# Three chained blocks: the first product of a stage runs on the unnormed input and the norm's factor is put on its results

## What is computed

```python
def rmsnorm(x, g):
    y = xf * lax.rsqrt(jnp.mean(xf * xf, axis=-1, keepdims=True) + EPS)
    return y * g

# block 1
h = rmsnorm(x, ln_in_g); proj = h @ w_in        # its first 2048 columns: conv_a
...
x = x + y @ w_out
x = rmsnorm(x, final_g)
# block 2
h = rms_norm(x, norm1_g); proj = h @ w_in_2     # its first 2048 columns: q (sa_q)
...
x = x + merged @ w_out_2
h2 = rms_norm(x, norm2_g)
ff = square(relu(h2 @ w_ff1))
x = x + ff @ w_ff2
x = rms_norm(x, final_g_2)
# block 3
h = rms_norm_3(x, g_pre); proj = h @ w_in_3     # r and k of the scan: rwkv_rk
...
```

## Time and profile before

| what | value |
|---|---|
| median of 3 runs | 4041.4 us (4035.34 to 4043.63) |
| profiled execution | 4041.27 us, its span 4039.3 us |
| TensorE / its weight loads busy | 96% / 94% of the span |
| VectorE / ScalarE busy | 61% / 44% |
| DMA | 636.69 MB, mean 158 GB/s |
| instructions | 86905 |

### The profile page before, as it was taken

One profiled execution on the slowest core, in us unless ns is written; L12 is line 12 of the kernel. 1 busy time (PEld: TensorE's weight loads), 2 busy tenths in 40 slices (PEclk: granted clock), 3 DMA queues, 4 the chain that ended last, 5 costly groups with the idle time before them and its releaser, 6 DMA issues. The chain is left out here.

```text
span 4039.3 us, 86905 instructions
## 1 busy us (share of the span) xinstructions
PE 3889.9 (96%) x36410; PEld 3805.7 (94%) x36410; DVE 2484.2 (61%) x3560; ACT 1787.6 (44%) x2267; POOL 0.2 (0%) x4
## 2 busy tenths in 40 slices
PE   7999999999999899999999999999899999999998
PEld 7999999999998899999998999999899888899897
DVE  4699966876646653667645545455647665666465
ACT  3444444444444443466344434343345433345643
POOL 0000000000000000000000000000000000000000
PEclk9999999999999998999999999999999999999999
DMA  5555545435555464544554555555554311134454
GB/s 175 175 182 185 180 137 178 139 123 190 183 170 167 160 202 169 167 155 158 167 188 156 184 181 184 180 185 180 174 195 154 113 44 45 44 116 142 154 188 135
DMA packets 99405, 636.69 MB, mean 158 GB/s; under 512 B 11152, under 2 KB 14608, under 8 KB 28752
## 3 DMA queue, kind: packets, MB, share of 16 engines
q1 hardware_dynamic: 99120, 632.57, 47.5%
HBM read 624.10 MB, written 8.42 MB: 157 GB/s over the span
## 5 line engine op out<-in xcount | busy, mean ns | idle before, releaser
L310 PE MATMUL ps_gemm<-arena_r,w_hi 128*128 128x256 f32 x16576 | 2198.5, 285 | 41.5 <-DVE arena_r L649 17.2
L310 PEld LDWEIGHTS ps_gemm<-arena_r,w_hi 128*128 128x128 f32 x16576 | 2080.5, 192 | 58.7 <-issue 40.8
L256 DVE TENSOR_TENSOR ring_r<-ring,w_hi 128x1024 fp32r<-128x1024 f32 (+3 forms) x1264 | 1415.9, 1125 | 1055.1 <-ACT w_hi L250 1047.1
L250 ACT ACTIVATE w_hi<-ring 128x1024 fp32r<-128x1024 f32 (+3 forms) x1264 | 1229.7, 978 | 1208.0 <-PE ps_gemm L310 966.1
L310 PE MATMUL ps_gemm<-arena_r,ring_r 128*128 128x256 f32 x8288 | 1188.2, 284 | 22.9 <-DVE ring_r L256 22.0
L310 PEld LDWEIGHTS ps_gemm<-arena_r,ring_r 128*128 128x128 f32 x8288 | 1077.3, 192 | 33.4 <-DVE ring_r L256 31.2
L307 PE MATMUL ps_gemm<-w_hi,arena_r 128*128 128x256 f32 (+1 forms) x1408 | 192.2, 287 | 1.0 <-ACT w_hi L250 0.9
L1224 DVE SCALAR_TENSOR_TENSOR arena<-arena,vecs (+15 forms) x480 | 192.5, 466 | 0.0
L307 PEld LDWEIGHTS ps_gemm<-w_hi,arena_r 128*128 128x128 f32 x1408 | 181.1, 197 | 2.4 <-ACT w_hi L250 1.8
L467 ACT ACTIVATE arena<-ps_gemm 128x512 f32 (+2 forms) x99 | 59.1, 597 | 235.8 <-PE ps_gemm L310 188.2
L488 ACT ACTIVATE act_tmp<-ps_gemm 128x512 f32<-128x512 f32 x78 | 46.5, 596 | 167.9 <-PE ps_gemm L310 167.8
(11 more groups left out here) (335 smaller groups left out, 2296.8 us busy)
## 6 DMA issues: line engine op xcount, KB each, us to landing
ring<-in_ff SPq DMA_DIRECT2D x128, 1024.0 KB, 5.0
ring<-in_w_out SPq DMA_DIRECT2D x48, 1024.0 KB, 5.1
ring<-in_gate SPq DMA_DIRECT2D x32, 1024.0 KB, 5.1
ring<-in_conv_a SPq DMA_DIRECT2D x16, 1024.0 KB, 5.1
ring<-in_conv_b SPq DMA_DIRECT2D x16, 1024.0 KB, 5.1
ring<-in_gla_v SPq DMA_DIRECT2D x16, 1024.0 KB, 5.1
ring<-in_conv_z SPq DMA_DIRECT2D x16, 1024.0 KB, 5.0
ring<-in_conv_out SPq DMA_DIRECT2D x16, 1024.0 KB, 5.1
```

The source lines that it names most:

```text
L250: nc.scalar.activation(w_hi[q % 2][:, 0:size], ring[slot][:, part], ACT.Copy).then_inc(hi_ready, 1)
L256: nc.vector.tensor_tensor(ring_lo[slot][:, part], ring[slot][:, part], w_hi[q % 2][:, 0:size].bitcast(F32), ALU.subtract).then_inc(lo_read ...
L310: mm = nc.tensor.matmul(bank[0:cw, 0:T], w[:, k * cols + c * cw:k * cols + (c + 1) * cw], r[:, kk, :], start=start, stop=stop)
```

## The change

It does the same at four places: the opening (conv_a), sa_q of block 2, ff1_0, and rwkv_rk of block 3.

- The first product there (the lead) runs on gain x input, without the factor per token. Its input is split beside the units of the product before (`feeds` in `Prod`: per unit two ScalarE copies with the gain as scale, two VectorE remainders), at the opening as x arrives.
- The factor is put on the results: kind "scaled" (VectorE, PSUM times the factor, 8 units each of conv_a, sa_q, rwkv_rk, in place of a ScalarE copy), or, in all 32 ff1 units, a second multiplication in "relu2" by 1 / (mean + eps).
- The sum matmuls (`add_up`) stand behind quarter 1 of the lead's unit 0, at the opening behind quarter 3.
- The normed and split input for the later products is made beside units 1 to 5 of the lead (`first_product`); the once-normed residual beside units 4 to 7. The feed-forward needs no normed input (`feed_forward`).
- Table loads of blocks 2 and 3 are issued behind the lead's weights. All stages are one program Block; tables are placed at fixed addresses.
- Each epilogue also waits for the epilogue before it (`bank_free`).

```diff
+                if s.feeds:
+                    act.wait_ge(bank_free, i2 + (s.g0 + j + 3))
+                    for c in range(2):
+                        x, hi = (b[:, bass.ds(2 * i2 + (2 * j + c), 1), :].rearrange("p a t -> p (a t)") for b in (s.dst, s.feeds[0]))
+                        a = nc.scalar.activation(hi, x, ACT.Identity, scale=s.feed_gain(2 * i2 + (2 * j + c)))
+                    a.then_inc(split_hi, 1)
                 if s.sums is not None:
...
+                if s.feeds:
+                    dve.wait_ge(split_hi, i2 + (s.split0 + j + 1))
+                    for c in range(2):
+                        x, hi, lo = (b[:, bass.ds(2 * i2 + (2 * j + c), 1), :].rearrange("p a t -> p (a t)") for b in (s.dst, *s.feeds[0:2]))
+                        a = nc.vector.scalar_tensor_tensor(out=lo, in0=x, scalar=s.feed_gain(2 * i2 + (2 * j + c)), in1=hi.bitcast(F32), op0=ALU.mult, op1=ALU.subtract)
+                    a.then_inc(split_done, 1)
...
+                if s.kind == "scaled":
+                    dve.wait_ge(quarters_done, 4 * i2 + (4 * (s.g0 + j) + 4))
+                    nc.vector.scalar_tensor_tensor(out=d, in0=ps, scalar=s.scale, in1=by_token(2), op0=ALU.mult, op1=ALU.mult).then_inc(bank_free, 1)
+                    return
...
                 elif s.kind == "relu2":
-                    last = nc.vector.tensor_tensor(d, t, t, ALU.mult)
+                    nc.vector.tensor_tensor(tmp2[slot][:, :, :], t, t, ALU.mult).then_inc(dve_mid, 1)
+                    dve.wait_ge(dve_mid, i2 + (s.mid0 + j + 1))
+                    last = nc.vector.tensor_tensor(d, tmp2[slot][:, :, :], by_token(2), ALU.mult)
...
+        def first_product(lead, then, gain, src, split, sums, factors, opening=None, mid=None, loads=(), dve_body=None):
...
                 @block.scalar
                 def _(act):
+                    if opening:
+                        opening.act(act)
+                    lead.act_part(act, 0, 0)
+                    lead.act_part(act, 0, 1)
+                    lead.act_part(act, 0, 2)
+                    lead.act_part(act, 0, 3)
                     root(act, b_in + 1, outer)
-                    parts.act(act)
-                    root(act, b_in + 2, inner)
-                    run.act(act)
+                    if mid:
+                        root(act, b_in + 2, inner)
+                    for u in range(1, lead.n):
+                        lead.act_part(act, u, 0)
+                        lead.act_part(act, u, 1)
+                        if 1 < u < 6:
+                            act.wait_ge(split_in, parts.made0 + u - 1)
+                            nc.scalar.activation(parts.hi(u - 2), parts.raw(u - 2), ACT.Copy).then_inc(split_hi, 1)
+                        lead.act_part(act, u, 2)
+                        lead.act_part(act, u, 3)
...
+                    for q in range(4):
+                        lead.pe_quarter(pe, 0, q)
+                        if q == 1 and not opening:
+                            sums.add_up(pe)
+                    if opening:
+                        opening.add_up(pe)
...
+                    lead.dve_part(dve, 0, 0)
+                    lead.dve_part(dve, 0, 1)
+                    lead.dve_part(dve, 0, 2)
+                    rest_of_weights(dve, 0, lead.g0 + 1, 1)
+                    dve.wait_ge(sums_done, b_sums + (1 if opening else 0))
...
+            def act(s, act):
+                act.sem_inc(bank_free, 2)
+                act.wait_ge(s.vecs_in, 16)
+                for q in range(4):
+                    act.wait_ge(s.x_in[q], 16)
+                    for c in range(4 * q, 4 * q + 4):
+                        x = nc.scalar.activation(s.split[0][:, c, :], s.x[:, c, :], ACT.Identity, scale=vcol(s.gain, c))
+                    x.then_inc(split_hi, 1)
+                    if q < 2:
+                        round_weights(act, 0, 0, q)
+                for q in range(4):
+                    nc.scalar.activation(s.squares[:, 4 * q:4 * q + 4, :], s.x[:, 4 * q:4 * q + 4, :], ACT.Square).then_inc(sq_ready, 1)
```

382 lines of the change are left out of this document (209 added, 173 removed).

## The result

The changed kernel takes 3986.42 us (median of 4 runs, 3984.14 to 3989.21), the kernel before 4041.33 us (4 runs, 4035.34 to 4043.63). The ratio is 0.9867 with a 95% interval of 0.985 to 0.9884. The forecast was 3990.6 us, 4.2 us too high. The profiled execution of the changed kernel took 3989.21 us, its span 3987.4 us, 51.9 us under the span before.

The account below looks back on a forecast made before the run. TensorE was taken to bound the kernel, its pauses at four places being what could go. Gains of 7.8 + 14.8 + 13.2 + 14.9 = 50.7 us off 4041.3 gave 3990.6 us, eight in ten within 3982 to 4001.

Parts of the forecast that it names:

- The reading of the profile: Whole kernel: TensorE busy 3889.9 of 4039.3 us, so only fewer matmuls or less of its 149 us standing still pay.
- Block 1 to 2 and 2 to 3: At sa_q and rwkv_rk: 17.6 and 17.7 us lost before, gains of 14.8 and 14.9 us after sums and one wait.
- The wait for the rest of unit 1's quarter 3: Unit 1 of sa_q: VectorE has this rest at +11.5, TensorE wants it at 10.56, so it waits 1.0 us.
- (a): Lead units too full: units 1 to 5 each make TensorE wait 1 us at three places; 4004 us, chance 0.11.
- (d): Sum matmuls wait for the last squares at the three later places, pause and slow clock partly return; 4005 us, chance 0.06.
- the table load: Root's table load in unit 1: 1.28 us by trace, 2.66 by the skill, making the wait 1.1 instead of 1.0 us.
- The feed-forward: At ff1_0: 14.1 us lost before, two sum matmuls of 0.9 us after, no root; gain 13.2 us.
- The cover of the 32 second multiplications: In the ff1 units: 0.69 us more ahead of quarter 1's rest leaves 1.0 us of cover, so it costs nothing.
- The opening: Unit 1 of conv_a starts at 38.7 instead of 46.48 us; gain 7.8 us, 5 to 10 with landings or second slow start.
- the landing of x2 and x3: In the opening, by bytes ahead in the queue: x2 lands at 15.4 us and x3 at 16.6.
- The tables' loads: Moved behind the 8 lead units on the sync queue; first reader six units later, so they cost nothing.
- the 50.7 us of the sum: Total gain at the four places: 7.8 + 14.8 + 13.2 + 14.9 us.

Follow-up runs that it names:

- the second (3988.89): The changed kernel run once more, unedited, to compare on one chip: 3988.89 us (3986.67 to 3994.19, 4 runs).

## Why the prediction was right, and where it wasn't

**The reading of the profile** held: only TensorE's idle time and its low clock were to be had, and they lay at the four places. One row was read for more than it shows: the 0.50 of the earlier trace rows belongs to a stretch in which TensorE stood (0.00 us busy). That the quarter behind it ran at this level shows in its length, 4.53 us (1402.35 to 1406.88) instead of 2.88.

**Block 1 to 2 and 2 to 3**, forecast 14.8 and 14.9 us net of one new wait. Measured 15.88 - 0.47 = 15.4 and 15.99 - 0.47 = 15.5. The chain was as worked out, step by step: the last squares added at T0 + 4.66 (4.75 forecast), sums at T0 + 5.76 without a wait, unit 1 at T0 + 13.24 (13.3), the clock at 1.00. The wait for the rest of unit 1's quarter 3 is where it was put and is the one term that was mis-sized: 0.47 us and not 1.0, because VectorE reached that rest at t1 + 9.65 instead of + 10.3. That it comes from the four scaled copies ahead of it is shown: moved behind it, both waits are gone. Part of the rivals' (a), that units 2 to 5 wait as well, didn't occur; (d), sums that wait for the squares, was made to occur by putting them one quarter, 2.88 us, earlier: more than the 1.1 us that they had to spare, and TensorE waited 1.67 us for them.

On the table load the prediction drew on the Trainium skill (ScalarE: Activation LUTs, section What ACT_TABLE_LOAD costs), and the trace decides against it:

```profile
1394.12 1.28 ACT L750 ACT_TABLE_LOAD   x1
...
1396.60 0.73 ACT L750 ACTIVATE stat<-stat 128x256 f32<-128x256 f32 x2 [1.19 <-DVE stat L977]
```

The load takes 1.28 us; the root starts 0.04 us behind its input (L977 ends at 1396.56). By the 2.66 us of the Trainium skill it couldn't have started before 1396.78.

**The feed-forward**, forecast 13.2, measured 13.2 in the trace and 13.3 when undone. The cover of the 32 second multiplications was put at 1.0 us and is 1.3.

**The opening**, forecast 7.8 (5 to 10), measured 10.0. The mechanism was right: the first quarter at 11.35 (11.5), the wait for quarter 2 behind the squares, the second slow start. The mis-sized term is the landing of x2 and x3: put at 15.4 and 16.6, but ScalarE began both at 14.20 and waited no more, so the squares (3.88 us for 4 x 1.06) ended at 21.3 instead of 23.0 and the wait was 3.20 us and not 5.0. Two slow quarters took 4.80 and 4.46. That the second was slow is partly luck: in two of nine profiles with this opening it wasn't.

**The tables' loads** were put at nothing, and that step failed. The prediction looked at when the load right behind the tables could start and at their first reader. It didn't add up the bytes of the queue: 2 MB of stores, 1.9 MB of tables, then the weights of unit 2 of rwkv_v. Before, the tables were loaded while TensorE stood at the boundary (it stood from 2885.16 to 2893.75; they were issued from 2885.44 and had landed by 2896.30), when nothing else was wanted. The pause that the change removed had been their cover. The new order costs 1.6 to 2.8 us in nine profiles, and nothing with the stores spread.

**Not foreseen at all** were the waits added to the epilogues (some 0.07 us in each of the short units) and the turn of the conv loop (2.3 us). Together with the rest of mem_out, whose cause stays open, they make block 1 4.2 us longer. So the 50.7 us of the sum meet 51.9 in the trace only because errors cancel: 3.5 us more at the four places than forecast (54.2 net of the wait in unit 1), 3.2 by chance at sa_wi and 1.4 in w_out_2's unit 0 and from rwkv_da to the end (0.7 of them by chance at the last sums), against 6.9 not counted (4.16 in block 1, 2.75 at rwkv_v). That the forecast of the time came within 4.2 us of the first median and within 1.7 of the second (3988.89) is therefore in part luck.

## What to carry to other kernels

When a change removes a pause, list what else used the pause: transfers that were free there now stand in a queue of bytes before something urgent. A norm's factor per token can be applied to a product's results; what it needs is one quarter's work between the last piece of the input and the sums, and an order on the helpers in which nothing long stands ahead of the piece that TensorE wants next. And a stretch far from the edit that changes by a repeatable microsecond may be a loop that lies elsewhere in the program: move the code by some tens of instructions before looking for another cause.

## What the runs showed of the hardware

TensorE's clock falls to 1.2 GHz not only behind pauses. In sa_wi, whose matmuls have 8 columns, TensorE is busy all the time and the granted clock still goes down to 0.50 for part of it (0.50 over 1556 to 1565 in the changed kernel), and how long differs between executions: the same stretch took 32.75, 34.36 or 35.97 us. In conv_out it goes down while TensorE makes 16 small matmuls (L1364, 16 rows, 4.56 us from 623.81), again without a pause: 11 of the 14 profiles have it, and conv_out to gate1 takes 99.0 to 99.1 us in them and 95.99 in the other three, in kernels with and without the change.

After pauses it isn't settled by their length alone either. Those of 4.2 to 5.9 us (at w_out_2, and in the scan of block 3) were followed by the low level in each profile. Those of 3.00 us (in block 1, the same instruction each time) were in 11 of 14, those of 2.38 us (also one instruction) in 5 of 14. At the opening 2.53 and 2.61 us were, 2.39 and 2.51 weren't. None of 1.67 us and none of those at rwkv_v (1.40 to 2.54 us) was.

The first quarter of all, 11.35 to 16.15, ran at half pace (3.75 us for 16 matmuls) while the profile gives a granted clock of 1.00 for it:

```profile
11.00:15.00 4.00, 3.65 (x17) 3.68 (x18) 4.00 (x7) 2.91 (x6) 0.00 (x0) 1.00 1.03 409
22.00:26.00 4.00, 3.61 (x17) 3.64 (x18) 2.36 (x2) 1.19 (x2) 0.00 (x0) 0.57 0.40 170
```

The second row, of the second slow quarter, does show it. So for these first microseconds the durations of the matmuls say more than the clock's column.
